# Two lines of ScalarE's step change places: exponentials ahead of a PSUM copy in the windowed attention of a decoder step

## The chip, the core and the metric

The kernel runs on 1 core of one Trainium2 chip. The metric is the device time of one execution in microseconds (us). All data are float32.

## The reference

One layer of a hybrid decoder is applied to 2048 prompt tokens and to 64 sample tokens. A combined input projection (1024 to 8720 columns) feeds two branches, and a gated output projection follows. The part that matters here is the first branch, softmax attention of three dilated windows with 8 heads of 64 each:

```python
s = einsum('bnqhd,bnkhd->bnhqk', qb, kk)      # blocks of 128 queries against the own and the previous block
s = where(mask, s, -inf)                      # band of the window, causal
m = max(s);  p = exp(s - m);  den = sum(p)
o = einsum('bnhqk,bnkhd->bnqhd', p / den, vv)
lse = m + log(den)
```

The second branch is a gated linear recurrence over chunks of 64 tokens. It makes decays from gates with exp and log, and then for each tile of 128 tokens a few small products and a state that is carried on.

## The kernel before

The projection comes first and ends at about 1487 us of the span. Its work is cut into slots, and every engine walks through the same list of steps q, two for each slot. From step FIRST_Q on only attention and recurrence are left, up to about 1930 us; then come the sample tokens' attention and the output projection.

**Attention.** There are 48 tasks. A task is one block of 128 queries of one window group and all 8 heads. It has four units of two heads each. Two units make a pair, and one pair starts at every even step, so there are 96 pairs. 21 tasks are "near": they have no previous block, and their scores are 128 wide for each head, not 256. For the pair that starts at step q, the engines do this, each in its own queue, in order:

- step q: TensorE makes the scores (L1722). VectorE adds the mask, scales, takes the row's extreme and writes to SBUF (mask_and_max, L1436). ScalarE takes the exponentials with their sums (exps, L1089), four activations for the pair; each unit of the pair is signalled by itself.
- step q+2: TensorE turns the exponentials over (transpose_p, L1733). ScalarE copies the first unit's transposed block from PSUM to SBUF (pT_evac, L1119), VectorE the second unit's (L1446).
- step q+4: TensorE multiplies them with the values (sums, L1746), after it has waited for both copies. When the task's last pair is summed, ScalarE copies the result out (o_evac, L1099).

The order within one step of TensorE is: scores of the new pair, sums of the pair two places back, one turning-over of queries or keys (L1702) if it is due, transpose_p of the pair one place back, then the recurrence's part. VectorE's order is: masks, evacuation of the turned queries or keys (L1416, L1410, or L1422 for a result), its pT_evac, then the recurrence's part. Masks of the next pair come behind all that. Scores of a pair wait until the pair before is masked.

**Recurrence.** It is spread over the same steps. There are four gate stretches, at about 1510, 1600, 1700 and 1800 us, each followed by four tiles of eight steps each. In a gate stretch ScalarE does log_sums (L1123 and L1125: exp, then log, of 128x1024, with an ACT_TABLE_LOAD ahead of the log and another ahead of the next exps), and some steps later decays and key_decays (L1131 to L1139, three more activations of 128x1024). These long activations are queued behind the step's attention work.

Buffers: sm has room for four units' scores, the transposed blocks have two PSUM banks and two SBUF buffers (pT), one for each unit of a pair. The step's order on each engine is written out by hand, in one function attend(q) for each.

Of the kernel before, what the change touches and what calls it, by code (L numbers as in the profile page):

```python
# [245 lines left out]
def project(nc, A, S, O, ident, sT, sn, gss, B, late_stage):  # L246
# [180 lines left out]
    score_at = {xs[0].q: xs for xs in pairs}  # L427
# [34 lines left out]
    with st:  # L462
# [221 lines left out]
        with nc.Block() as block:  # L684
# [323 lines left out]
            def _(act):  # L1008
# [75 lines left out]
                def exps(x):  # L1084
                    act.wait_ge(masked, x.u + 1)
                    o, lo = ends[:, x.i % 4, :], P if is_near(x) else 0
                    for h in range(2):
                        hh, y = 2 * x.c + h, sm[:, x.u % 4, h, lo:]
                        last = nc.scalar.activation(y, y, ACT.Exp, bias=o[:, hh:hh + 1], scale=-1.0,  # L1089
                                                    accum_out=o[:, NH + hh:NH + hh + 1])  # L1090
                    last.then_inc(exp_done, 1)

                def o_evac(i):
                    act.wait_ge(pv_done, last_unit(i).u + 1)
                    if i == 0:
                        act.wait_ge(mm_done, NSLOT)
                    if i >= 1:
                        act.wait_ge(o_moved, i)
                    nc.scalar.copy(oT[:, :, :], p_o[:, :, :]).then_inc(o_evacd, 1)  # L1099

                def ends_copy(i):
                    act.wait_ge(exp_done, last_unit(i).u + 1)
                    if i >= 2:
                        act.wait_ge(og_out[i % 2], 16 * (i // 2))
                    nc.scalar.copy(og[:, i % 2, CH:], ends[:, i % 4, :]).then_inc(o_turned, 1)

                def o_store(i):
                    act.wait_ge(o_turned, i + 1)
                    act.wait_ge(o_moved, i + 1)
                    act.dma_start(rows_in(tasks[i], OG[:, tasks[i].g, :]), og[:, i % 2, :]).then_inc(og_out[i % 2], 16)  # L1110

                def pT_evac(x):
                    b = slice(1, 4, 2) if is_near(x) else slice(0, 4)
                    act.wait_ge(pt_done, x.u + 1)
                    if x.u == 0:
                        act.wait_ge(mm_done, NSLOT)
                    if x.u >= 2:
                        act.wait_ge(pv_done, x.u - 1)
                    nc.scalar.copy(pT[:, x.u % 2, b, :], p_t2[x.u % 2][:, b, :]).then_inc(pt_evacd[0], 1)  # L1119
# [37 lines left out]
                def recur(q):  # L1157
                    if q - 2 in gates_of:
                        log_sums(gates_of[q - 2])
                    if q - 7 in gates_of:  # L1160
                        decays(gates_of[q - 7])
                    if q - 8 in gates_of:
                        key_decays(gates_of[q - 8])
                    if q - 3 in tile_of:
                        kd_evac(tile_of[q - 3])
                    if q - 7 in tile_of:
                        out_evac(tile_of[q - 7])
# [3 lines left out]
                def attend(q):  # L1171
                    if q in sum_at and sum_at[q][1].c == 3:
                        o_evac(sum_at[q][1].i)
                    if q in turn_p_at:
                        pT_evac(turn_p_at[q][0])
                    for x in score_at.get(q, ()):
                        exps(x)
                    if turn_qk_at.get(q, (0, 0))[1] == 2:
                        ends_copy(turn_qk_at[q][0])
                    if turn_qk_at.get(q - 2, (0, 0))[1] == 2:  # L1180
                        o_store(turn_qk_at[q - 2][0])
                    recur(q)
                    late_tail(q - LATE)
# [21 lines left out]
                for s in range(NSLOT + 3):  # L1205
                    if 1 <= s <= NSLOT:
                        evac(s - 1)
                    if s - 2 in gate_no:
                        gate(s - 2)
                    if s < NSLOT:  # L1210
                        if s in split_at:
                            split_hi(split_at[s])
                        attend(2 * s)
                        for c in conv_at.get(s - 1, ())[2 * (s == 1):] if s else ():
                            conv(c)
                        prepare(s)
                        attend(2 * s + 1)
                for q in range(FIRST_Q, LAST_Q):
                    attend(q)
# [1966 lines left out]
```

## Time and profile before

| | |
|---|---|
| median of 3 runs | 2412.43 us (2405.74 to 2415.95) |
| the profiled execution | 2415.95 us, its span 2414.2 us |
| TensorE busy | 2279.2 us, 94% of the span |
| VectorE busy | 1708.3 us, 71% |
| ScalarE busy | 806.2 us, 33% |
| mean granted TensorE clock | 0.979 |

"Busy" is the time in which an engine executes an instruction. A row of a timeline gives the start, the duration, engine, line, operation, what is written and read, and how many instructions of the kind were merged; in square brackets stands the idle time ahead of it and what ended that.

### The profile page before, as it was taken

To read this page: it belongs to the slowest core of one execution; us is meant where nothing else is said; L and a number is where in the kernel's file an instruction comes from. 1 tells how busy PE (TensorE), PEld (TensorE's weight loads), DVE (VectorE), ACT (ScalarE), POOL (GpSimd) and SP (SyncE) were. 2 spreads that over 40 slices of the span, in tenths; PEclk is the share of its full clock that TensorE was granted. 3 is DMA by queue.
4 is the path that set the end of the run, shared out by engine and by line. 5 is a ranking of instruction groups with operands and counts; after the bars stand their busy time and mean duration, and the time that the engine had idled before them with its cause. 6 is when DMAs were issued, how large, how long until landed. Compare 5 with 4: busy or idle time off the path is not lost. (4 is left out here: it accounts for less than half of the span.)

```text
span 2414.2 us, 36166 instructions
## 1 busy us (share of the span) xinstructions
PE 2279.2 (94%) x12996; PEld 1839.5 (76%) x12996; DVE 1708.3 (71%) x3345; ACT 806.2 (33%) x1705; POOL 277.2 (11%) x455
## 2 busy tenths in 40 slices
PE   6999999987999999999999998889899897999998
PEld 4887878866788888888878886667777646888887
DVE  5855767856775688888868886778888757655653
ACT  4332221112223422222122233676767524122221
POOL 1000011221210012212121220001010010000000
PEclk8999999998999999999999999899999999999999
DMA  8999999999996666888787797665555398434431
GB/s 255 244 278 319 274 287 276 254 248 244 298 268 213 202 197 225 271 257 265 253 249 241 250 322 262 216 211 191 174 194 170 113 293 327 160 128 170 154 148 70
DMA packets 271184, 553.40 MB, mean 229 GB/s; under 512 B 33392, under 2 KB 60480, under 8 KB 268896
## 3 DMA queue, kind: packets, MB, share of 16 engines
q1 hardware_dynamic: 200688, 358.77, 44.1%
q0 software_dynamic: 58000, 166.36, 26.5%
q10 hardware_dynamic: 12320, 25.96, 2.8%
q8 instruction: 106, 1.74, 0.3%
q14 instruction: 70, 0.57, 0.1%
HBM read 442.60 MB, written 191.50 MB: 263 GB/s over the span
## 5 line engine op out<-in xcount | busy, mean ns | idle before, releaser
L1633 PE MATMUL b_acc<-b_whi,a_hi 128*128 128x512 f32 x1792 | 706.4, 394 | 28.5 <-ACT b_u L1062 15.1
L1635 PE MATMUL b_acc<-b_whi,a_lo 128*128 128x512 f32 x1792 | 701.3, 391 | 0.0
L1634 PE MATMUL b_acc<-b_wlo,a_hi 128*128 128x512 f32 x1792 | 701.2, 391 | 0.0
L1633 PEld LDWEIGHTS b_acc<-b_whi,a_hi 128*128 128x128 f32 x1792 | 338.7, 189 | 101.3 <-ACT b_u L1062 15.5
L1045 ACT CAST b_whi<-b_w 128x2048 fp32r<-128x2048 f32 (+1 forms) x127 | 228.6, 1801 | 546.3 <-PE b_acc L1635 380.8
L1635 PEld LDWEIGHTS b_acc<-b_whi,a_lo 128*128 128x128 f32 x1792 | 338.5, 189 | 71.5
L1634 PEld LDWEIGHTS b_acc<-b_wlo,a_hi 128*128 128x128 f32 x1792 | 338.8, 189 | 68.9
L1295 DVE TENSOR_TENSOR b_wlo<-b_w,b_whi 128x2048 fp32r<-128x2048 f32 (+1 forms) x127 | 273.1, 2151 | 83.1 <-ACT b_whi L1045 82.9
L1089 ACT ACTIVATE c_sm<-c_sm,c_ends 128x256 f32<-128x256 f32 (+1 forms) x384 | 172.4, 453 | 9.5 <-DVE c_ends L1436 9.5
L1436 DVE CUSTOM_DVE_ANT_0 c_sm<-c_p_s,c_mask 128x256 f32<-128x256 f32 (+1 forms) x384 | 117.1, 361 | 39.3 <-PE c_p_s L1722 38.6
L970 POOL DMA_DIRECT2D a_x<-tm x188 | 107.2, 574 | 285.9 <-DVE sT L1402 217.5
L1402 DVE TENSOR_REDUCE sT<-a_x 128x8 f32<-128x512 f32 x167 | 114.6, 686 | 5.8
L2396 PE MATMUL f_p_b<-w_wb_hi,f_bT_hi 128*128 128x512 f32 x256 | 102.1, 399 | 7.9 <-DVE f_bT_lo L2945 4.9
L1722 PE MATMUL c_p_s<-c_kT,c_qT 64*128 64x128 f32 x1200 | 93.2, 290 | 11.0 <-DVE c_ends L1436 9.9
L2398 PE MATMUL f_p_b<-w_wb_hi,f_bT_lo 128*128 128x512 f32 x256 | 100.3, 392 | 0.0
L2397 PE MATMUL f_p_b<-w_wb_lo,f_bT_hi 128*128 128x512 f32 x256 | 100.1, 391 | 0.0
L1722 PEld LDWEIGHTS c_p_s<-c_kT,c_qT 64*128 64x128 f32 x1200 | 76.4, 190 | 28.7 <-issue 28.1
L959 POOL DMA_DIRECT2D b_ck<-in_cache_kv_w x96 | 52.7, 549 | 376.3 <-DVE sT L1402 374.1
L2396 PE MATMUL f_p_z<-w_wo_hi,f_mT_hi 128*128 128x512 f32 x240 | 94.8, 395 | 0.0
L2398 PE MATMUL f_p_z<-w_wo_hi,f_mT_lo 128*128 128x512 f32 x240 | 93.5, 390 | 0.0
L1746 PE MATMUL c_p_o<-c_pT,c_v 128*64 128x128 f32 x1200 | 89.8, 287 | 3.8 <-ACT c_pT L1119 2.7
L2397 PE MATMUL f_p_z<-w_wo_lo,f_mT_hi 128*128 128x512 f32 x240 | 93.4, 389 | 0.0
(373 smaller groups left out, 3477.3 us busy)
## 6 DMA issues: line engine op xcount, KB each, us to landing
b_w<-t SPq DMA_DIRECT2D x64, 1024.0 KB, 8.1
t<-in_w_in POOLq DMA_DIRECT2D x48, 1024.0 KB, 10.9
b_w<-in_w_in SPq DMA_DIRECT2D x47, 1024.0 KB, 8.0
a_x<-tm POOLq DMA_DIRECT2D x167, 256.0 KB, 6.8
tm<-b_st SPq DMA_DIRECT2D x128, 256.0 KB, 7.0
b_ck<-in_cache_kv_w POOLq DMA_DIRECT2D x96, 256.0 KB, 5.1
c_qk<-tm SPq DMA_DIRECT2D x96, 256.0 KB, 3.6
t<-t POOLq DMA_DIRECT2D x16, 1024.0 KB, 12.3
```

The source lines that it names most:

```text
L1045: nc.scalar.copy(whi[:, b % HI_RING, part, 0:w], w_raw[:, k, part, 0:w]).then_inc(w_hi, 1)
L1089: last = nc.scalar.activation(y, y, ACT.Exp, bias=o[:, hh:hh + 1], scale=-1.0, accum_out=o[:, NH + hh:NH + hh + 1])
L1295: V.tensor_tensor(wlo[:, k, part, 0:w], w_raw[:, k, part, 0:w], whi[:, b % HI_RING, part, 0:w].bitcast(F32), ALU.subtract).then_inc(w_lo, 1)
L1402: V.tensor_reduce(out, y.rearrange("p (h e) -> p h e", h=NH), AX_X, ALU.add).then_inc(scored, 1)
L1436: last = V.tensor_tensor_reduce(out=sm[:, x.u % 4, h, lo:], in0=p_s[:, h, at + lo:at + 2 * P], in1=mask[:, lo:], scale=-HD ** -0.5, scalar ...
L1633: nc.tensor.matmul(out, stat_hi, mov_hi, start=first, stop=False)
L1634: nc.tensor.matmul(out, stat_hi, mov_lo, start=False, stop=False)
L1635: return nc.tensor.matmul(out, stat_lo, mov_hi, start=False, stop=last)
L1722: last = nc.tensor.matmul(p_s[:, h, at:at + P], qT[r, x.i % 2, x.c, :], kT[r, n % KEPT, x.c, :], start=True, stop=True)
L2396: nc.tensor.matmul(out, stat_hi, mov_hi, start=first, stop=False)
L2397: nc.tensor.matmul(out, stat_hi, mov_lo, start=False, stop=False)
L2398: return nc.tensor.matmul(out, stat_lo, mov_hi, start=False, stop=last)
```

## The change

In ScalarE's attend(q) the call of pT_evac for the pair one place back and the calls of exps for the new pair change places. Nothing else changes: the same instructions with the same waits run on every engine.

```diff
                 def attend(q):
                     if q in sum_at and sum_at[q][1].c == 3:
                         o_evac(sum_at[q][1].i)
+                    for x in score_at.get(q, ()):
+                        exps(x)
                     if q in turn_p_at:
                         pT_evac(turn_p_at[q][0])
-                    for x in score_at.get(q, ()):
-                        exps(x)
                     if turn_qk_at.get(q, (0, 0))[1] == 2:
                         ends_copy(turn_qk_at[q][0])
```

## Rows read from the trace of the kernel before

**Rows 1.** The page, part 1: busy time, share of span, instructions.
```profile
PE 2279.2 (94%) x12996; PEld 1839.5 (76%) x12996; DVE 1708.3 (71%) x3345; ACT 806.2 (33%) x1705; POOL 277.2 (11%) x455
```
**Rows 2.** Busy time in stretches: PE, PEld, DVE, ACT, POOL, clock, DMA.
```profile
1800.00:1850.00 50.00, 44.90 (x538) 37.78 (x536) 43.77 (x135) 39.37 (x117) 2.10 (x3) 1.00 0.47 152
1850.00:1900.00 50.00, 48.41 (x630) 41.51 (x630) 39.24 (x132) 31.91 (x110) 3.24 (x5) 1.00 0.33 109
```
**Rows 3.** Waits from 1500 to 1920 us: total us, times, longest.
```profile
ACT c_pT L1119 <- PE c_p_t L1733: 84.9, 76, 3.0
PE c_p_o L1746 <- ACT c_pT L1119: 2.7, 2, 1.4
PE c_p_t L1733 <- ACT c_sm L1089: 1.2, 4, 0.3
```
**Rows 4.** Group of one line and shape, same stretch: busy us, mean ns.
```profile
L1089 ACT ACTIVATE c_sm<-c_sm,c_ends 128x256 f32<-128x256 f32 x212 | 105.1, 499 | 4.2 <-DVE c_ends L1436 4.2
```
**Rows 5.** Timeline among tiles, 1780 to 1785 us: DVE, ACT, PE.
```profile
1780.41 0.41 DVE L1436 CUSTOM_DVE_ANT_0 c_sm<-c_p_s,c_mask 128x256 f32<-128x256 f32 x1
...
1781.44 0.58 ACT L1119 COPY c_pT<-c_p_t 128x512 f32<-128x512 f32 x1 [0.43 <-PE c_p_t L1733]
...
1784.44 1.09 PE L1746 MATMUL c_p_o<-c_pT,c_v 128*64 128x128 f32 x16
```
**Rows 6.** Timeline of ACT in the fourth gate stretch.
```profile
1808.49 1.28 ACT L1089 ACT_TABLE_LOAD   x1
...
1818.64 0.21 ACT L1131 ACTIVATE d_decay<-d_ge 128x16 f32<-128x16 f32 x1
...
1821.70 0.56 ACT L1099 COPY c_oT<-c_p_o 128x512 f32<-128x512 f32 x1
```
**Rows 7.** Timeline of PE, fourth gate stretch.
```profile
1808.66 1.09 PE L1746 MATMUL c_p_o<-c_pT,c_v 128*64 128x128 f32 x16
...
1811.91 0.66 PE L1733 MATMUL c_p_t<-ident,c_sm 128*128 128x128 f32 x4 [0.33 <-ACT c_sm L1089]
...
1823.24 1.09 PE L1746 MATMUL c_p_o<-c_pT,c_v 128*64 128x128 f32 x16
```
**Rows 8.** Timeline of DVE, fourth gate stretch.
```profile
1812.86 0.68 DVE L1446 COPY c_pT<-c_p_t 128x512 f32<-128x512 f32 x1
...
1815.85 0.42 DVE L1436 CUSTOM_DVE_ANT_0 c_sm<-c_p_s,c_mask 128x256 f32<-128x256 f32 x1
```
**Rows 9.** Timeline of DVE, the same mask in the first three stretches.
```profile
1527.11 0.28 DVE L1436 CUSTOM_DVE_ANT_0 c_sm<-c_p_s,c_mask 128x128 f32<-128x128 f32 x1
...
1613.83 0.29 DVE L1436 CUSTOM_DVE_ANT_0 c_sm<-c_p_s,c_mask 128x128 f32<-128x128 f32 x1
...
1714.28 0.42 DVE L1436 CUSTOM_DVE_ANT_0 c_sm<-c_p_s,c_mask 128x256 f32<-128x256 f32 x1
```
**Rows 10.** Timeline of PE, the sums that answer to 1823.24 there.
```profile
1533.60 0.66 PE L1746 MATMUL c_p_o<-c_pT,c_v 128*64 128x128 f32 x8 [1.32 <-ACT c_pT L1119]
...
1620.48 0.66 PE L1746 MATMUL c_p_o<-c_pT,c_v 128*64 128x128 f32 x8
...
1721.67 1.09 PE L1746 MATMUL c_p_o<-c_pT,c_v 128*64 128x128 f32 x16
```
**Rows 11.** Timeline of PE: the gates' first product.
```profile
1509.14 2.07 PE L1761 MATMUL c_p_g<-d_glr,d_wa 32*128 32x512 f32 x4 [9.47 <-DMA d_glr<-gl]
```
**Rows 12.** Timeline of PE and ACT at the end of the attention.
```profile
1910.71 1.97 PE L1746 MATMUL c_p_o<-c_pT,c_v 128*64 128x128 f32 x16
...
1920.20 0.66 PE L1746 MATMUL c_p_o<-c_pT,c_v 128*64 128x128 f32 x8
...
1920.40 0.51 ACT L1089 ACTIVATE c_sm<-c_sm,c_ends 128x256 f32<-128x256 f32 x1 [1.75 <-DVE c_ends L1436]
...
1923.05 0.59 ACT L1119 COPY c_pT<-c_p_t 128x512 f32<-128x512 f32 x1
...
1924.09 0.41 ACT L2525 ACTIVATE e_s<-e_s,e_nm 128x136 f32<-128x136 f32 x1 [0.45 <-DVE e_wd L2760]
```

## The prediction

> **What bounds the kernel now.** I read the page's first part, then the stretches of time, then the waits of the attention's stretch, and last the timelines of single steps. TensorE is busy for 94% of the span and ScalarE for a third [rows 1], so the reader should start from TensorE. The edit touches only steps from FIRST_Q on, because neither a pair nor a turned block exists before, so only about 1487 to 1930 us can move. Where the recurrence works on its tiles, TensorE does 48.4 of 50 us; where a gate stretch falls in, 44.9 [rows 2]. The list of waits looks inviting: ScalarE's copy (L1119) waited 84.9 us in 76 places for the turned block, and exps stand behind it. But time of ScalarE is not time of the kernel. What matters is whether TensorE waited for ScalarE: 2.7 us in 2 places for the copy, 1.2 us in 4 places for the exponentials [rows 3]. So at most 3.9 us of these waits can be won, and the question is what the copy, now behind four activations, makes late.
>
> **What is moved.** Nothing is added or removed. In each of 96 steps the copy goes behind exps of the next pair. An activation of 256 columns takes 0.50 us [rows 4], starts overlap a little, and four with their last sum take 2.07 us when the starts in the timeline are 0.49 apart; four of 128 columns take 1.65 us. The copy takes 0.58 us (0.37 near). Exps may start when the first unit is masked, which is 0.8 us after the mask's first start (two masks of 0.42 us that overlap, and a read), 0.5 us near. The copy is wanted by sums one step later, in front of transpose_p; exps only by transpose_p. So exps get earlier where nobody waits for them, and the copy gets later where somebody may. Neither of the two issues a DMA; ScalarE's stores stand behind both and are as late as the step is. Behind sums in TensorE's queue stand the turning of queries or keys and transpose_p; VectorE's evacuation and its own copy wait for these, and the next mask stands behind them.
>
> **Among the tiles: nothing.** Take the step at 1780 us [rows 5]. The mask starts at 1780.41, so its first unit is ready at 1781.23. The result's copy is done by then, so exps run from 1781.2 to 1783.3 and the copy ends at 1783.8. Sums start at 1784.44, so 0.64 us are to spare. I did this for every pair among tiles. The margins come out at 0.35 to 1.2 us with a few of 0.1 to 0.2, and none is below zero by more than 0.1. The cover is the recurrence's work in TensorE's queue between transpose_p and the next sums; without it the margin would be gone, and that is what happens in the gate stretches.
>
> **A gate stretch, the fourth.** ScalarE's long activations end where the copy L1119 stood, and a table load follows.
> 1. The table load starts at 1808.49 [rows 6], and now with no copy ahead of it (but with one 0.6 us late from the step before) it starts at about 1808.5 as well. Exps of 256 columns follow from 1809.8 to 1811.9, the copy ends at 1812.4, and sums that began at 1808.66 [rows 7] begin at 1812.5, 3.85 us later.
> 2. Before, transpose_p waited for the same exps (its second half began at 1811.91 [rows 7] and ended at 1812.57), so part is given back. Now it ends at 1.1 (sums) + 0.5 (turning) + 1.0 after 1812.5, at about 1815.05: 2.5 us late.
> 3. VectorE's copy of the second unit at 1812.86 [rows 8] goes to 1815.15, 2.3 us late, and with it two scans and the mask at 1815.85, which becomes 1818.15.
> 4. The first unit is then ready at 1819.0. Exps 2.07, the copy 0.55, and only then the decays, which began at 1818.64 [rows 6]: now 1821.6. The copy used to be done before them. The decays take until 1821.70 in before, 3.05 us; now until 1824.65. Then 0.48 for the result's copy, 2.07 for exps, 0.55 for the copy: 1827.8. Sums began at 1823.24 [rows 7] and begin 4.6 us late.
>
> After this the margins among the tiles return, and TensorE, which is the bound there, has nothing with which to catch up. So 4.6 us stay.
>
> **The other three.** The same steps put VectorE 1.3, 1.2 and 1.4 us late there, since these are nearer to each other at the first stall (near or mixed pairs, or half clock). With step 4 from their masks [rows 9]: first stretch, 1527.11 + 1.3 + 0.5 + 1.65 + 0.35 + 3.05 + 0.48 + 1.65 + 0.37 = 1536.5 against 1533.60, of which transpose_p's own old wait of about 0.2 is given back: 2.7. Second, 1613.83 + 1.2 and the same terms: 1623.1 against 1620.48: 2.6. Third, 1714.28 + 1.4 + 0.8 + 2.07 + 0.55 + 3.05 + 0.48 + 2.07 + 0.58 = 1725.3 against 1721.67: 3.6 [rows 10].
>
> **Both ends.** Three stalls of about 0.7 to 1.3 us before 1500 us cost nothing: TensorE waits there 9.5 us for a load that hangs on the projection's stores and not on ScalarE [rows 11]. At the end the last pair's exps run from 1920.4 to 1922.4 either way, but the copy of the pair before now follows them, with the sample's copies after it, and sums that began at 1920.20 begin at 1923.0. Transpose_p ends 1.8 us late, the last copy (1923.05) starts at 1924.75, and ScalarE's exps of the samples behind it at 1925.25, not at 1924.09 [rows 12]. These are on the chain to what follows: 1.15 us. The stage after starts from loads that wait for the attention's last stores, so it moves as a whole.
>
> **The sum.** 2.7 + 2.6 + 3.6 + 4.6 + 1.15 = 14.7 us. The profiled execution took 2415.95 us and would take 2430.6; it was the slowest of the three runs, 3.5 us over their median of 2412.43. Against the median the forecast is 2427 us, 0.6% slower. From below the price is bound by the first stalls being wholly hidden by VectorE, from above by TensorE's clock, which are rivals below. A measurement of this kernel can tell about 0.5%, 12 us.
>
> **Rivals.**
> - *It is not slower.* Exps start up to 1 us earlier, and the loop from transpose_p over the copy to the next exps is gone, so ScalarE runs ahead and reaches the gates' activations early. The place is the gate stretches; the price is a gain of 3.9 us (all waits of TensorE for ScalarE [rows 3]), 2408.5. It decides if exps of the next pair can begin before the long activations that stand between. Against it: the order in the queue is fixed, and in the fourth stretch the long ones start later, not earlier, since the copy is now just ahead of them. 0.06.
> - *VectorE hides it.* In the gate stretches VectorE has three long operations too. If the first stall doesn't reach its masks, step 4 keeps only 2.0 to 2.6 us of each stretch without the shift of 1.2 to 2.3: 14.7 - 6.2 = 8.5, 2421. For it: masks there wait for VectorE's own queue. Against: its copy is queued ahead of the scans and waits for transpose_p. With everything hidden it is 2412. Together 0.26.
> - *The clock falls.* TensorE now stands still for about 3 us in one place of each stretch. At 1.2 GHz sixteen products took 1.97 us [rows 12] and at 2.4 GHz 1.09 [rows 7]. A step has about four such groups, so up to 3.5 us for each slowed step; half of it beside waits, four stretches: 7 us more, 2434. For it: the last attention pairs ran at that level after TensorE had waited. Against it: the fourth stretch has TensorE busy for only 44.9 of 50 us and kept a clock of 1.00 [rows 2]. 0.12. The Trainium skill ("TensorE: Matmul & The Clock Gate", section "HAM oscillation — how this bites in real kernels") says that idle gaps of the matmul engine throttle its clock again, so that the work after each wait starts slow; that speaks for this rival and against the change, which would by that rule give the 2434.
> - *The margins among the tiles don't hold.* With 1 us more for each copy, most of the 65 pairs there would lose about 0.3 us: 20 us more, 2447. Nothing in the rows speaks for handovers that slow. 0.02.
> - The forecast, 12 to 18 us: 0.54.
>
> **Numbers.** The likeliest case alone spans 2424 to 2431. The range reaches down into the hidden case and up to the clock's: 2412 to 2436 leaves out about 2 in 10. Slower by over 0.5% (above 2424.5): most of the forecast, the clock and the margins, 0.62. Within 0.5%: the hidden cases, the small gain and the forecast's lower edge, 0.36. Faster by over 0.5% has no mechanism with that price: 0.02.
>
> **What the changed kernel's profile would show.** ScalarE's waits of L1119 for L1733 fall from 84.9 us to a small number, since the block is long turned when the copy's turn comes, and ScalarE waits for masks (L1436) in its place. TensorE's wait of L1746 for L1119 rises from 2.7 us to about 15 us or more, in 10 to 15 places, all next to gates' activations and none among tiles. The wait of L1733 for L1089 vanishes. The fourth stretch is about 4.6 us longer, a tile stretch is unchanged. I would be wrong if TensorE's waits for the copy stay under 6 us, if they appear among the tiles, or if they grow as forecast and the end of the attention doesn't move.

## The result, and the profile after

The changed kernel took 2432.27 us (median of 5, 2424.39 to 2436.36), the kernel before 2409.12 (median of 5, 2404.47 to 2415.95) in the same comparison: ratio 1.0093, 95% interval 1.0070 to 1.0114. It is slower, by 23 us in the medians. The forecast was 2427, range 2412 to 2436. More executions narrow this down: 22 of the changed kernel on record have a median of 2431.6, and in three later comparisons the kernel before has 2411.9 (23 runs), 2412.1 (7) and 2414.3 (13). So the loss is rather 17 to 20 us, and 3 us or more of the 23 are the luck of five runs each.

First the page's part 1 of the changed kernel, with the line above it. It answers to [rows 1].

```profile
span 2424.6 us, 36166 instructions
...
PE 2282.9 (94%) x12996; PEld 1845.8 (76%) x12996; DVE 1708.9 (70%) x3345; ACT 806.1 (33%) x1705; POOL 276.4 (11%) x455
```

Every engine has the same instructions as before, and ScalarE and VectorE the same busy time. TensorE's is 3.7 us longer with the same 12996 recorded products, the first hint that some of them ran at a lower clock. The span is only 10.4 us longer. In this execution the projection happened to end 9.1 us earlier (the first mask started at 1479.6 us, in the one before at 1488.7). Over all fourteen traces of this study, in none of which the projection was touched, that moment lies anywhere from 1479.6 to 1492.0. So the single spans say little, and the parts between fixed points say much.

The next view gives busy time in stretches (PE, PEld, DVE, ACT, POOL, granted clock, DMA) and answers to [rows 2].

```profile
1800.00:1850.00 50.00, 41.33 (x472) 35.52 (x470) 37.09 (x111) 34.14 (x100) 0.62 (x1) 0.93 0.34 109
1850.00:1900.00 50.00, 47.62 (x596) 40.62 (x592) 41.60 (x140) 31.95 (x110) 4.58 (x7) 1.00 0.43 147
```

The stretch with a gate stretch in it has TensorE busy for 41.3 us where it had been 44.9, and the clock there fell from 1.00 to 0.93. The waits from 1500 to 1925 us (total, times, longest) answer to [rows 3]:

```profile
ACT c_oT L1099 <- PE c_p_o L1746: 81.0, 40, 11.9
ACT c_sm L1089 <- DVE c_ends L1436: 69.1, 54, 3.6
...
PE c_p_o L1746 <- ACT c_pT L1119: 22.2, 11, 3.2
...
ACT c_pT L1119 <- PE c_p_t L1733: 2.5, 3, 1.2
```

ScalarE's wait for the turned block went from 84.9 to 2.5 us. That is the gain which the order promises, and it bought nothing: longer waits in front of the exponentials (69.1 us) and of the result's copy (81.0 us) stand in its place. In the kernel before, those two were:

```profile
ACT c_oT L1099 <- PE c_p_o L1746: 44.3, 35, 13.0
ACT c_sm L1089 <- DVE c_ends L1436: 7.7, 7, 3.2
```
TensorE's wait for ScalarE's copy went from 2.7 us in 2 places to 22.2 us in 11. Its wait at L1733 for L1089 is gone from the list.

Among the tiles nothing moved. The step of [rows 5] in the changed kernel's timelines of DVE, ACT and PE, 0.56 us later as a whole:

```profile
1780.97 0.42 DVE L1436 CUSTOM_DVE_ANT_0 c_sm<-c_p_s,c_mask 128x256 f32<-128x256 f32 x1
...
1783.77 0.56 ACT L1119 COPY c_pT<-c_p_t 128x512 f32<-128x512 f32 x1
...
1785.00 1.09 PE L1746 MATMUL c_p_o<-c_pT,c_v 128*64 128x128 f32 x16
```

The copy started at 1781.44 and starts at 1783.77 now. It used to wait for the turned block and now stands behind exps, and the sums begin 4.03 us after the mask, as before. Between the copy's end (1784.33) and the sums 0.67 us are left; 0.64 had been forecast.

The fourth gate stretch is another matter. ACT's timeline, against [rows 6]:

```profile
1809.06 1.28 ACT L1089 ACT_TABLE_LOAD   x1
1810.35 0.51 ACT L1089 ACTIVATE c_sm<-c_sm,c_ends 128x256 f32<-128x256 f32 x1
...
1812.33 0.56 ACT L1119 COPY c_pT<-c_p_t 128x512 f32<-128x512 f32 x1
...
1822.94 0.56 ACT L1119 COPY c_pT<-c_p_t 128x512 f32<-128x512 f32 x1
1823.41 0.23 ACT L1131 ACTIVATE d_decay<-d_ge 128x16 f32<-128x16 f32 x1
...
1826.48 0.57 ACT L1099 COPY c_oT<-c_p_o 128x512 f32<-128x512 f32 x1
...
1828.93 0.57 ACT L1119 COPY c_pT<-c_p_t 128x512 f32<-128x512 f32 x1
```

and PE's, against [rows 7]:

```profile
1812.95 1.69 PE L1746 MATMUL c_p_o<-c_pT,c_v 128*64 128x128 f32 x16 [2.96 <-ACT c_pT L1119]
1814.57 1.11 PE L1702 MATMUL c_p_qk<-ident,c_qk 128*128 128x128 f32 x4
1815.47 1.65 PE L1733 MATMUL c_p_t<-ident,c_sm 128*128 128x128 f32 x8
1817.05 1.16 PE L1722 MATMUL c_p_s<-c_kT,c_qT 64*128 64x128 f32 x16
...
1829.55 1.24 PE L1746 MATMUL c_p_o<-c_pT,c_v 128*64 128x128 f32 x16 [1.93 <-ACT c_pT L1119]
1830.72 1.12 PE L1702 MATMUL c_p_qk<-ident,c_qk 128*128 128x128 f32 x4
1831.63 1.91 PE L1733 MATMUL c_p_t<-ident,c_sm 128*128 128x128 f32 x8
```

Read the two together. Ahead of the sums TensorE stands still for 2.96 us, because the copy that they need ended at 1812.9 behind a table load and four activations. 17 us later it stands still again, behind the decays. And look at the durations. The turning-over of eight blocks took 1.65 and 1.91 us. In the kernel before, the next one in this stretch took

```profile
1815.11 1.04 PE L1733 MATMUL c_p_t<-ident,c_sm 128*128 128x128 f32 x8
```

The view by stretches shows why (the last column but two is the clock; 0.50 is 1.2 GHz):

```profile
1813.30:1816.70 3.40, 3.40 (x24) 3.07 (x21) 0.78 (x3) 2.02 (x8) 0.00 (x0) 0.50 0.02 5
1818.20:1822.20 4.00, 2.50 (x30) 2.09 (x28) 3.97 (x12) 1.24 (x5) 0.00 (x0) 1.00 0.50 185
1830.40:1833.80 3.40, 3.40 (x21) 3.08 (x16) 0.92 (x2) 1.77 (x7) 0.00 (x0) 0.50 0.03 5
```

Behind each of the two waits TensorE ran at 1.2 GHz, and between them it was back at 2.4. VectorE's copy and mask of this stretch, against [rows 8]:

```profile
1817.16 0.69 DVE L1446 COPY c_pT<-c_p_t 128x512 f32<-128x512 f32 x1 [0.75 <-PE c_p_t L1733]
...
1820.16 0.42 DVE L1436 CUSTOM_DVE_ANT_0 c_sm<-c_p_s,c_mask 128x256 f32<-128x256 f32 x1
```

The end of the attention, PE, then ACT, then the view by stretches, against [rows 12]:

```profile
1930.54 1.98 PE L1746 MATMUL c_p_o<-c_pT,c_v 128*64 128x128 f32 x16 [2.73 <-ACT c_pT L1119]
1932.44 1.97 PE L1733 MATMUL c_p_t<-ident,c_sm 128*128 128x128 f32 x8
```

```profile
1933.60 0.59 ACT L1119 COPY c_pT<-c_p_t 128x512 f32<-128x512 f32 x1 [2.41 <-PE c_p_t L1733]
1934.08 0.41 ACT L2525 ACTIVATE e_s<-e_s,e_nm 128x136 f32<-128x136 f32 x1
```

```profile
1930.50:1935.50 5.00, 4.96 (x32) 4.30 (x34) 1.84 (x10) 2.59 (x14) 0.00 (x0) 0.50 0.02 7
```

**A ruler for all runs.** To compare parts whatever the projection did, I number the pairs by the start of their first mask (L1436) and take the time from pair n's to pair m's. The first column is the kernel before, in us; the others are differences from it. "Tiles" are the three tile parts between the gate stretches (pairs 13 to 26, 34 to 48 and 57 to 70; before 48.69, 65.22 and 59.44 us) and the one behind the fourth (79 to 92, 62.8), together. "Rest" is from pair 95's mask to the end of the span.

| pairs | before | after | e1 | e2 | e3 | e4 | e5 | e6 | e7 | e9 | e10 |
|---|---|---|---|---|---|---|---|---|---|---|---|
| 5 to 13 | 31.86 | +3.92 | +2.23 | -0.33 | +2.50 | -2.20 | -0.67 | +1.85 | +1.50 | +1.98 | +1.30 |
| 26 to 34 | 33.76 | +2.65 | +4.46 | -0.06 | +1.89 | -1.63 | -0.77 | +2.69 | +0.46 | +1.08 | -0.07 |
| 48 to 57 | 41.68 | +4.10 | +4.56 | -0.24 | +1.06 | +0.58 | -0.37 | +5.54 | +2.19 | +3.52 | +0.08 |
| 70 to 79 | 42.59 | +7.18 | +7.00 | 0.00 | +3.05 | -0.35 | +0.99 | +4.84 | +1.98 | +4.90 | +0.30 |
| the four | 149.9 | +17.9 | +18.3 | -0.6 | +8.5 | -3.6 | -0.8 | +14.9 | +6.1 | +11.5 | +1.6 |
| tiles | 236.2 | 0.0 | 0.0 | 0.0 | 0.0 | 0.0 | 0.0 | +11.1 | +12.0 | 0.0 | 0.0 |
| rest | 494.6 | +2.9 | +0.2 | +1.0 | +0.5 | -0.1 | +2.8 | +3.7 | -1.1 | +1.1 | +0.5 |

The tile parts agree to 0.02 us each where the table says 0.0. The four gate stretches took 17.9 us more; the forecast had 13.5 for them.

How well does one trace tell a gate stretch? The kernel e1 below has the changed order in the gate stretches, as the changed kernel has. Its first two stretches differ from that kernel's by 1.7 and 1.8 us, in opposite directions, its last two by 0.5 and 0.2, and the sum of the four by 0.4. So a single one of the first two is uncertain by some 2 us; the fourth and the sum are much better. The split of each stretch into TensorE's idle and busy time (from the view by stretches, between the same two masks; idle is the length less the busy time) says why:

| pairs | idle: before | after | e1 | busy: before | after | e1 |
|---|---|---|---|---|---|---|
| 5 to 13 | 6.44 | 9.48 | 9.03 | 25.43 | 26.30 | 25.07 |
| 26 to 34 | 7.26 | 10.07 | 10.43 | 26.50 | 26.33 | 27.78 |
| 48 to 57 | 4.63 | 8.74 | 9.29 | 37.05 | 37.03 | 36.95 |
| 70 to 79 | 4.31 | 8.67 | 8.49 | 38.28 | 41.09 | 41.10 |
| the four | 22.6 | 37.0 | 37.2 | 127.3 | 130.8 | 130.9 |

The instructions of TensorE in a stretch are the same in all three, so a clearly longer busy time means slower work: in the fourth stretch it goes with a mean clock of 0.93 where the kernel before has 1.00. Of the 17.9 us some 14.3 are idle time, close to the forecast's 13.5, and 3.5 are slower work, for which the forecast has nothing. The two rows of the fourth stretch, before and after:

```profile
1794.58:1837.17 42.59, 38.28 (x452) 31.56 (x449) 38.21 (x113) 33.40 (x99) 1.98 (x3) 1.00 0.46 153
1795.14:1844.90 49.76, 41.09 (x452) 34.53 (x449) 38.48 (x112) 33.20 (x99) 1.53 (x3) 0.93 0.39 129
```

### The profile page after: what moved, and what is told of

Read it like the earlier page. It is cut to its first block and busy times, and to the rows that moved or that the text cites. A ratio compares the mean times of both kernels' runs of the same rounds, so it can differ in the third digit from the quotient of the medians.

```text
span 2424.6 us, 36166 instructions
## 1 busy us (share of the span) xinstructions
PE 2282.9 (94%) x12996; PEld 1845.8 (76%) x12996; DVE 1708.9 (70%) x3345; ACT 806.1 (33%) x1705; POOL 276.4 (11%) x455
## 5 line engine op out<-in xcount | busy, mean ns | idle before, releaser
L1295 DVE TENSOR_TENSOR b_wlo<-b_w,b_whi 128x2048 fp32r<-128x2048 f32 (+1 forms) x127 | 273.0, 2150 | 69.1 <-ACT b_whi L1045 68.9
L1089 ACT ACTIVATE c_sm<-c_sm,c_ends 128x256 f32<-128x256 f32 (+1 forms) x384 | 172.5, 451 | 71.1 <-DVE c_ends L1436 70.6
L1436 DVE CUSTOM_DVE_ANT_0 c_sm<-c_p_s,c_mask 128x256 f32<-128x256 f32 (+1 forms) x384 | 117.1, 362 | 38.8 <-PE c_p_s L1722 38.1
L1746 PEld LDWEIGHTS c_p_o<-c_pT,c_v 128*64 128x64 f32 x1200 | 67.0, 142 | 39.9 <-ACT c_pT L1119 30.1
## 6 DMA issues: line engine op xcount, KB each, us to landing
t<-in_w_in POOLq DMA_DIRECT2D x48, 1024.0 KB, 11.1
t<-t POOLq DMA_DIRECT2D x16, 1024.0 KB, 11.5
```

The costliest lines, as they stand in the source:

```text
L1295: V.tensor_tensor(wlo[:, k, part, 0:w], w_raw[:, k, part, 0:w], whi[:, b % HI_RING, part, 0:w].bitcast(F32), ALU.subtract).then_inc(w_lo, 1)
L1436: last = V.tensor_tensor_reduce(out=sm[:, x.u % 4, h, lo:], in0=p_s[:, h, at + lo:at + 2 * P], in1=mask[:, lo:], scale=-HD ** -0.5, scalar ...
L1746: last = nc.tensor.matmul(p_o[HD * h:HD * (h + 1), x.c, :], v[:, n % KEPT, cols], pT[:, x.u % 2, 2 * h + b, :], start=(b == 1 if near else ...
```

## The experiments

**Which steps.** Theory 1 (the queue): the loss comes from steps in which a long activation or a table load is queued with the copy behind exps. Two kernels take the change apart by place, a third puts the copy between the two units' exps.

```diff
+late_copy = any(g - 1 <= q <= g + 12 for g in g_at.values())   # e2_rest: not any(...)
+if q in turn_p_at and not late_copy:
+    pT_evac(turn_p_at[q][0])
 for x in score_at.get(q, ()):
     exps(x)
-if q in turn_p_at:
+if q in turn_p_at and late_copy:
     pT_evac(turn_p_at[q][0])
```

> The new order holds only in the steps of the four gate stretches, from one step before the gates to twelve after; the 9 steps at the start, the tiles' steps and the last ones have the old order. Theory 1 (the copy comes late behind the exponentials only where ScalarE has long activations, and TensorE waits for it): the attention from its first mask to its last takes 444 to 448 us, as in the changed kernel (447.5), against 430.9 in the kernel before; TensorE waits 15 to 24 us for the copy; the ratio to the kernel before is 1.006 to 1.010. Rival (the loss is spread over all pairs, the tiles' too): not more than half of it is left, 438 us or less and a ratio under 1.004. Theory 2 (the stage behind the attention lost 2.9 us because the last pairs' steps are late): that stage takes 494.6 us as in the kernel before, not 497.5.

> The converse: the old order in the steps of the four gate stretches, the new order in all others, the last pairs' among them. Theory 1: the attention takes 430 to 433 us, TensorE waits for the copy under 6 us before 1900 us, the ratio is 0.999 to 1.002. Rival (spread over all pairs): at least half of the 16.6 us are here, 439 us or more. Theory 2: the stage behind the attention takes about 497 us here.

```diff
-for x in score_at.get(q, ()):
+for x in score_at.get(q, ())[0:1]:
     exps(x)
 if q in turn_p_at:
     pT_evac(turn_p_at[q][0])
+for x in score_at.get(q, ())[1:]:
+    exps(x)
```

> In every step the copy stands between the two units' exponentials: behind the first unit's, ahead of the second's. Theory 1: each wait of TensorE for the copy is shorter by the two activations that now follow it (1.0 us, 0.8 near), and the decays start with the same queue ahead of them as in the changed kernel. Four stretches lose 0.5 to 3 us each, and the attention takes 436 to 443 us, between the kernels. Rival (it is not the length of the queue ahead of the copy that counts, but that it is behind exps at all, for instance since ScalarE then starts them earlier and misses a handover): as the changed kernel, 446 us or more.

Late in the gate steps alone: 2430.63 us against 2411.94, ratio 1.0069 (1.0048 to 1.0090), the four stretches +18.3. Late everywhere else: 2413.80, ratio 1.0010 (0.9995 to 1.0025), the four stretches -0.6. Between: 2419.50, ratio 1.0022 (1.0006 to 1.0038), +8.5. TensorE's wait for the copy, from the lists of waits (1470 to 1910 us) of the three in this order (the sums' line has a number of its own in each):

```profile
PE c_p_o L1749 <- ACT c_pT L1119: 22.6, 12, 3.1
```

```profile
PE c_p_o L1749 <- ACT c_pT L1119: 2.8, 4, 0.9
```

```profile
PE c_p_o L1748 <- ACT c_pT L1119: 16.9, 8, 3.2
```

So the loss is nearly all in the 14 steps around each gates' call. Elsewhere e2 shows 1.0 us at the end, which is less than the 2.9 of the changed kernel; its last stage took 495.6 us where about 497 had been expected (more on this below), and its attention 429.0, where 430 to 433 had been. With two activations ahead of the copy instead of four about half is lost. The third line is a warning: 16.9 us of wait is seven tenths of the 23.7 that the changed kernel has in the same window, and the stretches lose half. A sum of waits doesn't add up to time, since part of each stall is given back behind it.

**Is it the long activations?** The next two keep the order of every instruction and make the gates' activations short (one column for each of the blocks in place of all, and an exponential in place of the logarithm, so that no table is loaded). One is made from the kernel before, the other from the changed one.

```diff
-nc.scalar.activation(ge[1][:, :, :], ge[1][:, :, :], ACT.Exp).then_inc(gate_step, 1)
+nc.scalar.activation(ge[1][:, :, 0:1], ge[1][:, :, 0:1], ACT.Exp).then_inc(gate_step, 1)
...
-nc.scalar.activation(ge[1][:, :, :], ge[1][:, :, :], ACT.Ln, bias=1.0).then_inc(gate_step, 1)
+nc.scalar.activation(ge[1][:, :, 0:1], ge[1][:, :, 0:1], ACT.Exp).then_inc(gate_step, 1)
```

(and the same in decays and key_decays, but for the activation of 128x16 at L1131, which keeps its size and gets the other sign in its scale)

> The kernel before, with the recurrence's five activations of 128x1024 in each gate stretch cut to one column and the log replaced by exp, so that no table is loaded; the gates and decays are therefore not computed as the reference has them, all else is. Old order. Theory 1: TensorE's few waits for ScalarE go away and VectorE's for the log too; the attention takes 424 to 430 us. It is the base for the next run.

> The changed kernel with the same cut: activations of one column, no log and no table load; gates and decays are not the reference's. Theory 1 (the long activations and the table load make the copy late): the difference to the run with the old order and the same cut falls from 16.6 us to 1 to 6 us, what is left being the pairs that have no work of the recurrence between transpose_p and the sums (0.5 to 1.3 us each, one or two in each stretch). Rival (the missing cover alone makes the loss, the long activations don't matter): the difference stays at 12 us or more.

One run each: 2406.88 us for the old order, 2416.49 for the new. In the four stretches the new order costs -0.8 + 3.6 = 2.8 us over the old one, not 17.9. The wait for the copy in the new order:

```profile
PE c_p_o L1746 <- ACT c_pT L1119: 8.6, 14, 0.8
```

No single wait is longer than 0.8 us. The two single times differ by more, 9.6 us: 4.6 by where the projection ended, 2.1 in the attention and 2.9 behind its last mask. So the copy behind exps does little harm by itself. It takes the long ones, the table load among them, in the same queue to push it past the sums. Which part each of them has was not separated.

**Does TensorE's queue give it back?** If sums are what waits, turning queries and keys ahead of them should use the time. First in every step, then in the gate steps alone, each in the new and the old order.

```diff
 for x in score_at.get(q, ()):
     scores(x)
+if q in turn_qk_at:              # the second pair of kernels: and only in gate steps
+    transposes(*turn_qk_at[q])
 for x in sum_at.get(q, ()):
     sums(x)
-if q in turn_qk_at:
-    transposes(*turn_qk_at[q])
```

> The changed kernel, and TensorE does the turning of queries and keys (L1702) ahead of sums and not behind them, so that its wait for the copy overlaps 0.5 us of other work and VectorE gets its block without waiting for sums. Theory 1: each of the waits in a gate stretch (3 to 4) costs 0.5 us less, and VectorE's masks are less late: the attention takes 438 to 444 us, not 447.5. Rival (the clock makes most of the loss, since TensorE runs at 1.2 GHz after each wait): the idle time shrinks little, the slow stretches stay, 446 us or more.

> The kernel before with the same change of TensorE's order. There it waits only 2.7 us for the copy, so theory 1 expects 0 to 4 us less, 427 to 431 us of attention and a ratio of 0.998 to 1.001: the gain of the run above is a part of the loss given back and not a better order by itself. If it gained 6 us or more, VectorE's late blocks would have been a bound of their own that neither theory names.

> The changed kernel, and TensorE does the turning of queries and keys ahead of sums only in the gate stretches' steps, where no block of the recurrence's keys stands in the same bank. The run with this order everywhere lost since the turning waits there for ScalarE's copy of that block, 12.8 us in 16 places. Theory 1: without that the four stretches lose about 0.5 us for each of their 3 to 4 waits less than in the changed kernel, 10 to 14 us in place of 17.9, and the parts between them are as before. Rival: as much as in the changed kernel.

> The same of TensorE on the kernel before. Theory 1: 0 to 3 us less than the kernel before in the four stretches, since VectorE gets its block 0.5 to 1 us earlier in stretches where it is the one that is late; ratio 0.998 to 1.000. If it is faster by more than its interval it beats both kernels.

Turned first in every step: 2440.64 us (ratio 1.0123, 1.0107 to 1.0138) in the new order and 2428.73 (1.0077, 1.0061 to 1.0094) in the old. Both forecasts failed: the attention took 456.3 us where the theory had 438 to 444, and in the old order 449.2 us where 427 to 431 had been expected. The first number lies where the rival had put it (446 or more), but not for the rival's reason, the clock. The gate stretches of the new order are 3 us better than without, and the tile parts, untouched by anything so far, are 11 to 12 us worse. The waits of the new-order kernel name the reason:

```profile
PE c_p_qk L1702 <- ACT d_kdT L1145: 12.8, 16, 1.3
...
PE c_p_o L1746 <- ACT c_pT L1119: 10.0, 10, 1.6
```

The turning writes a PSUM bank which ScalarE must first have read (L1145), once a tile, 16 times in all. Behind the sums no such wait is in the changed kernel's list; ahead of them it shows. In the gate steps alone there is no such wait: 2421.55 us (one run) and +11.5 in the four stretches, so 6.4 of the 17.9 us are given back. In the old order it is 2412.13 against 2414.29, ratio 0.9989 (0.9971 to 1.0007): no difference that can be measured. Its four stretches are 1.6 us longer, not 0 to 3 us shorter as expected, nearly all in the first, which is within that stretch's scatter. So no version of this study that computes the reference's result beats the kernel before.

**The extra of the fourth stretch.** Forecast 4.6 us, measured 7.2. Theory 2: the clock adds it, since two 1.2 GHz stretches stand behind the two waits. The rival is that the queue costs more than I summed. To keep TensorE at work without touching any order, unread products of 128 columns into the gates' PSUM bank are put ahead of the sums in the fifth and eleventh step of each gate stretch.

```diff
+for k, g in g_at.items():
+    for _ in range({5: 18, 11: 12}.get(q - g, 0)):   # e11: 9 and 6; e12: 13 and 9
+        pe.wait_ge(gate_step, G_STEPS * k + 4)
+        nc.tensor.matmul(p_g[:, 0, 0:P], ident[:, :], ident[:, :], start=True, stop=True)
 for x in sum_at.get(q, ()):
     sums(x)
```

> The changed kernel with products added that nobody reads (128x128, into the gates' PSUM bank while it is not in use): 18 ahead of the sums five steps after each gates' step, where TensorE waits 2.96 us, and 12 ahead of the sums eleven steps after, where it waits 1.93 us. They fill most of the wait. Theory 2 (what the four stretches lost beyond the forecast, 17.9 us against 13.5, comes from TensorE's clock, which falls to 1.2 GHz after such a wait): no stretch at 1.2 GHz lies between pairs 70 and 79, and that part is 44.6 to 48.0 us long (49.8 in the changed kernel, 42.6 before), though work was added; between pairs 48 and 57 45 us. Rival (the extra is VectorE's and ScalarE's queues alone, the clock is beside the path): 49.5 us or more there.

It took 2430.35 us (ratio 1.0058, 1.0039 to 1.0077), and the fourth stretch +7.65, 50.24 us where 44.6 to 48.0 had been expected; the third took 46.6, not 45. Taken by the number alone this speaks for the rival. But the timeline of its PE shows that the filling was itself late:

```profile
1815.86 4.29 PE L1826 MATMUL c_p_g<-ident 128*128 128x128 f32 x36
1820.08 1.09 PE L1746 MATMUL c_p_o<-c_pT,c_v 128*64 128x128 f32 x16
```

The copy (it started at 1816.81 and took 0.56) was there at 1817.4, and the sums began 2.7 us after it, with no idle time in front of them. So this run had put a new delay in the place of the clock's, and its clock fell all the same (0.95 in the table below). The test was made again with less.

> The changed kernel with 9 unread products ahead of the sums in the first stalled step of each gate stretch and 6 in the second, half of what the filled kernel had. There the 36 recorded halves of the first filling took 4.29 us and the sums of the fourth stretch began 2.7 us after the copy they need had ended, so the filling itself was late. Half of it takes about 2.1 and 1.4 us and fits into the waits of 2.96 and 1.93 us. Theory that the clock makes the extra of the fourth stretch: no 1.2 GHz stretch there, and it takes 47.0 to 48.0 us between its first and last mask instead of the changed kernel's 49.8 (before 42.6, forecast 47.2). Rival, that the extra is the queue's: 49.3 to 50.3 us although the clock stays up. If the clock falls all the same, the run tells nothing on this.

> As the half filling, with 13 and 9 products: about 3.1 and 2.2 us, a little longer than the waits. By the clock theory the fourth stretch takes 0.5 to 1.5 us longer than with the half filling if the clock stays up in both, so 47.5 to 49.5 us, and shorter than that kernel if its clock falls and this one's does not. By the rival it is at 49.8 or above in both.

| | 5 to 13 | 26 to 34 | 48 to 57 | 70 to 79 | the four | clock in 1800 to 1835 |
|---|---|---|---|---|---|---|
| before | 31.86 | 33.76 | 41.68 | 42.59 | 149.9 | 1.00 |
| after | +3.92 | +2.65 | +4.10 | +7.18 | +17.9 | 0.90 |
| e8, 18 and 12 | +2.75 | +3.32 | +4.92 | +7.65 | +18.6 | 0.95 |
| e11, 9 and 6 | +1.69 | +2.24 | +3.04 | +4.77 | +11.7 | 0.95 |
| e12, 13 and 9 | +1.69 | +2.24 | +3.25 | +4.39 | +11.6 | 1.00 |

PE's timeline in the fourth stretch of the kernel with 13 and 9 products, and under it the view of 1800 to 1835 us:

```profile
1809.31 3.17 PE L1826 MATMUL c_p_g<-ident 128*128 128x128 f32 x26
1812.41 1.09 PE L1746 MATMUL c_p_o<-c_pT,c_v 128*64 128x128 f32 x16
1813.44 0.66 PE L1702 MATMUL c_p_qk<-ident,c_qk 128*128 128x128 f32 x4
1813.93 1.04 PE L1733 MATMUL c_p_t<-ident,c_sm 128*128 128x128 f32 x8
...
1825.39 2.27 PE L1826 MATMUL c_p_g<-ident 128*128 128x128 f32 x18
1827.60 1.09 PE L1746 MATMUL c_p_o<-c_pT,c_v 128*64 128x128 f32 x16
```

```profile
1800.00:1835.00 35.00, 31.26 (x346) 26.98 (x344) 28.34 (x82) 26.69 (x76) 0.00 (x0) 1.00 0.31 98
```

The same view of the changed kernel:

```profile
1800.00:1835.00 35.00, 26.50 (x280) 22.88 (x276) 25.55 (x72) 24.60 (x68) 0.00 (x0) 0.90 0.31 102
```

With 26 and 18 recorded products (two records for each) TensorE kept 2.4 GHz, and the stretch took 46.98 us. Nothing of the order was undone, and the sums behind the first stall began no earlier (17.9 us after pair 70's mask, 17.8 in the changed kernel), yet 2.8 us of the extra are gone. That is what the clock had cost there, and the split above has the same numbers without any filling: 2.8 us more of busy time, 4.4 more of idle time. What is left, 4.4 us, is the queue's part, and 4.6 was its forecast. The rival (49.3 to 50.3 us) is out. The run with 9 and 6 products took 47.36 us, inside its range, but its clock was down once, ahead of the first stall, and by its own terms it then tells nothing on this. For 13 and 9 two cases had been named: 47.5 to 49.5 us if the clock stayed up in both, and shorter than the kernel with 9 and 6 if only that one's clock fell. The second came about. All this is one trace of each kernel.

By the four stretches both kernels are 6 us faster than the changed one, for adding work that nobody reads. Their one run each took 2420.94 and 2420.73 us, beside 2416.04 for the kernel before. The same filling in the kernel before was not run. It has stretches at 1.2 GHz of its own in the first three gate stretches, and the filling keeps the clock up there too (0.99, 1.00 and 1.00 between the masks with 13 and 9 products). So +1.69, +2.24 and +3.25 are not the queue's part alone: they also hold a gain that the kernel before might have had. Only in the fourth, where the kernel before has a full clock throughout, is the comparison clean.

## Why the prediction was right, point by point

**The mechanism and the place were right.** No gain came from the wait of 84.9 us. TensorE's wait for the copy rose to 22.2 us in 11 places ("about 15 us or more, in 10 to 15 places"), all in the gate stretches. The wait of L1733 for L1089 vanished, and ScalarE waits for masks instead. The tile parts are unchanged to 0.02 us, so the margins hold, the small ones too, and the rival of 2447 us is out. That it might be no slower (2408.5) is out as well: ScalarE did not reach the gates' activations early, the first long one of the fourth stretch started 0.5 us later (1805.61 - 0.56 against 1804.59). That VectorE hides it is out: its mask was late in the first stall, not less than forecast but more.

**The steps of the fourth stretch, measured.** Ahead of the stall the changed kernel's times are 0.56 us later than those before (the same mask at 1802.36 and 1801.80), so I take 0.56 off.
1. The sums were to begin 3.85 us late. 1812.95 - 0.56 - 1808.66 = 3.7. Right.
2. Transpose_p was to end 2.5 us late, with 1.1, 0.5 and 1.0 us for sums, turning and itself. They took 1.69, 1.11 and 1.65, and the end is at 1817.12: 4.0 late. This is the term that was mis-sized, by 1.5 us. I had priced everything behind the wait at 2.4 GHz.
3. The mask was to be 2.3 us late. 1820.16 - 0.56 - 1815.85 = 3.8 in the changed kernel. In the one with 13 and 9 products, which keeps its clock, the same mask is 2.2 us late.
4. The decays, the result's copy, four exponentials and the copy take as long as summed. From the mask at 1820.16 to the sums at 1829.55 are 9.4 us; from the forecast's 1818.15 to 1827.8 are 9.65. So the sums are 5.8 us late and not 4.6, by what came out of step 2. Then 1.2 GHz follows once more, and 7.2 us stay. With the clock up the whole is 4.4.

**The other three.** The sums of [rows 10] begin 3.0, 2.7 and 4.1 us late once the shift of each stretch's start is taken off; 2.9, 2.6 and 3.6 were forecast for them. The first stretch then lost 3.9 in all and not 2.7. Between the two masks the clock's mean is nearly the same before and after in these three (0.88 and 0.87, 0.90 and 0.91, 0.96 and 0.96), so there the clock adds little on the whole. It does fall in other places: in the first stretch it is down from 1526.5 us on, behind the sums, where the one before had its low piece ahead of them. By the split above 0.9 of the 3.9 us is longer busy time. In e1, with the same order, the first stretch loses 2.2 and the second 4.5, so this piece falls now here, now there, and the 1.2 us over the forecast are within that scatter.

**The end.** Forecast 1.15 us. The sums begin 3.41 us after the last pair's mask, exactly as summed (1923.0 - 1919.59). But they and transpose_p took 1.98 and 1.97 us, against 1.09 for the sixteen products of [rows 5] and for the eight blocks at the same place before, and the samples' exponentials (L2525) start 6.95 us after the mask (1927.13). It was 4.50 before and 5.66 by the forecast. So 2.45 late, 1.3 more than forecast: again the clock, which stood at 1.2 GHz from 1930.5 us on. The other traces bear this out. Among the kernels with the full change at this place, the clock's mean in the 10 us from the last mask is 0.66 in three (the changed one, e5, e6), and their rest is 2.8 to 3.7 us longer; it is 0.83 in five (e2, e8, e9, e11, e12), and theirs is 0.6 to 1.5 us longer. That is why e2 missed its 497 us: it has the wait but less of the slow clock. With the old order there the rest lies between -1.1 and +0.6, so it is no finer ruler than about 1 us.

**The clock's rival.** I gave it 0.12 and 7 us on top. It came true in part: about 2.8 us in the fourth stretch and 1.3 at the end, 4 of the 7, beside the forecast's waits and not in their stead. It did not come in each of the four stretches, as I had priced it. What I held against it was the fourth stretch before, with TensorE busy for 44.9 of 50 us at a full clock. TensorE's longest idle time there from 1806 to 1826 us is 1.87 us, so that row could say nothing on what one of 2.96 would do. The 2434 us of the rival is nearer to the measured 2432.3 than the forecast's 2427, and the range held the result partly because it had been drawn up to this rival's price. The Trainium skill ("TensorE: Matmul & The Clock Gate", section "HAM oscillation — how this bites in real kernels") says that gaps in the matmul stream throttle the clock and that the work behind each starts slow. The trace agrees for the waits of 2.96, 1.93 and 2.73 us shown above, and not for the second stretch's (below).

**The total.** By the parts, the changed kernel takes 16.6 us more between the first and the last mask (447.5 against 430.9) and 2.9 behind it, 19.5 us; by the medians 23.2, with an interval of 17 to 27 from the ratio, and 17 to 20 by all executions on record. So the parts and the many runs agree, and the 23 are partly chance. Against the forecast's 14.7 the 4.8 more are 2.6 in the fourth stretch, 1.2 in the first, 0.5 in the third and 1.75 behind the attention, less 1.3 for the pairs up to 5 and from 92 on, where the load's wait takes up what it can. Two waits for the copy stand before 1500 us (0.7 and 0.8 us), not three, and they cost nothing, as forecast.

## What to carry to other kernels

In an in-order queue, an instruction on which the bounding engine waits stands ahead of work that nobody needs soon, even if it looks idle there. The wait it spends on its own producer is not the cost; the time its consumer waits for it is. Before moving it, look at the longest work that ever shares the queue with it, since a margin of 0.6 us in most steps says nothing of the few that have a table load or a long activation in them. And when a new wait of 2 or 3 us of TensorE is priced, price the work behind it at 1.2 GHz as well, as a second sum. Afterwards split each stretch into the engine's idle and busy time: here the first was the queue's part and the second the clock's.

## What the runs showed of the hardware that was not expected

- Unread work made a kernel faster: 22 products in two places of the fourth stretch kept TensorE at 2.4 GHz behind both, and the stretch took 46.98 us instead of the changed kernel's 49.76.
- A wait's length alone doesn't tell whether the clock falls. In the changed kernel's second stretch PE waited 2.69 us at 1616.95 and the eight products and turnings behind it ran at the full clock. A wait of 1.94 us in the third stretch (1722.22) has the full clock behind it, the one of 1.93 in the fourth has not. And in the fourth stretch of the kernel with 9 and 6 products the clock was down behind a wait of only 0.63 us, where the changed kernel, with the same wait at 1805.76, had it up:

```profile
1616.95 0.66 PE L1746 MATMUL c_p_o<-c_pT,c_v 128*64 128x128 f32 x8 [2.69 <-ACT c_pT L1119]
1617.54 0.66 PE L1702 MATMUL c_p_qk<-ident,c_qk 128*128 128x128 f32 x4
```

```profile
1804.16 1.85 PE L1746 MATMUL c_p_o<-c_pT,c_v 128*64 128x128 f32 x16 [0.63 <-ACT c_pT L1119]
```

- The first of these kernels' stages ended anywhere within 12 us (1479.6 to 1492.0) with the same instructions, while the tile parts behind it repeat to 0.02 us. The gate stretches don't repeat so well (up to 1.8 us each with the same order), because the low pieces of the clock fall in different places; their sum repeats to 0.4. So parts between fixed points, from one trace each, tell more than medians of five runs, once it is known how well each part repeats.
